# Sums over heads on TensorE: eight products dealt to four column strips

## What is computed

```python
kk = heads(k * k_k)
kk = kk / jnp.maximum(jnp.sqrt(jnp.sum(kk * kk, axis=-1, keepdims=True)), 1e-12)
...
mean = jnp.mean(y, axis=-1, keepdims=True)
var = jnp.mean(jnp.square(y - mean), axis=-1, keepdims=True)
y = ((y - mean) * lax.rsqrt(var + RWKV_LN_EPS)).reshape(bsz, seq, W) * ln_w + ln_b
bonus = jnp.sum(r * k * r_k, axis=-1, keepdims=True) * v
```

## Time and profile before

| what | before |
|---|---|
| time, median of 3 runs | 2844.51 us (2843.17 to 2844.96) |
| span of the profiled execution | 2846.5 us |
| TensorE busy, matmuls | 2803.9 us (99%) x17275 |
| VectorE busy | 1735.5 us (61%) |
| ScalarE busy | 1315.8 us (46%) |
| mean granted TensorE clock | 0.997 |
| instructions of `head_sum` (L804) | 64 matmuls, 64 weight loads |

### The profile page before, as it was taken

How to read it: one execution, slowest core, us unless ns; L and a number is a source line. 1 busy time by engine, 2 the same in 40 slices (tenths; PEclk the granted TensorE clock), 3 DMA queues, 4 the chain that set the end, 5 groups by cost and what they waited for, 6 DMA issues and landing times.

```text
span 2846.5 us, 40996 instructions
## 1 busy us (share of the span) xinstructions
PE 2803.9 (99%) x17275; PEld 2398.9 (84%) x17275; DVE 1735.5 (61%) x2053; ACT 1315.8 (46%) x1672; POOL 43.6 (2%) x71
## 2 busy tenths in 40 slices
PE   8999899999999999999999999999999999999998
PEld 7888788788888888888888888888888888888886
DVE  5688666654445555555555666655666756665665
ACT  6445333544434443444434545644554444443444
POOL 2000000000000000000000100000000000000001
PEclk9999999999999999999999999999999999999999
DMA  7565214555545656655666555555456555555553
GB/s 232 177 193 176 77 47 150 186 182 192 179 135 183 186 192 192 191 193 183 197 190 189 189 180 190 178 169 174 161 180 198 185 195 190 187 198 192 190 181 132
DMA packets 392420, 504.60 MB, mean 177 GB/s; under 512 B 11360, under 2 KB 285293, under 8 KB 391213
## 3 DMA queue, kind: packets, MB, share of 16 engines
q1 hardware_dynamic: 385149, 490.35, 53.5%
q10 hardware_dynamic: 7088, 11.62, 1.3%
HBM read 499.77 MB, written 2.17 MB: 176 GB/s over the span
## 4 chain that ended last, share of the span: by engine, by line
PE 95%; DVE 3%; ACT 1%; issue 1%; DMA 0%; ACTq 0%; SPq 0%; DVEq 0%
PE PS L639 37%; PE PS L644 33%; PE PS L648 17%; PE PS L864 3%; PE PS L676 1%; DVE wlo L1889 1%; PE PS L996 0%; PE PS L1012 0%; PE PS L804 0%; PE PS L784 0%; PE PS L1045 0%; DMA slab<-in_x 0%; ACT whi L1287 0%; PE PS L819 0%; PE PS L1036 0%
## 5 line engine op out<-in xcount | busy, mean ns | idle before, releaser
L1889 DVE TENSOR_TENSOR wlo<-raw,whi 128x1024 fp32r<-128x1024 f32 x922 | 1127.0, 1228 | 791.1 <-ACT whi L1287 787.5
L1287 ACT ACTIVATE whi<-raw 128x1024 fp32r<-128x1024 f32 x922 | 970.3, 1057 | 963.3 <-PE PS L648 497.9
L644 PE MATMUL PS<-XX,whi 128*128 128x512 f32 (+1 forms) x3856 | 1216.8, 397 | 0.0
L648 PEld LDWEIGHTS PS<-XX,wlo 128*128 128x128 f32 (+1 forms) x3856 | 724.5, 188 | 171.3
L648 PE MATMUL PS<-XX,wlo 128*128 128x256 f32 (+1 forms) x3856 | 759.7, 278 | 0.0
L639 PE MATMUL PS<-whi,act 128*128 128x512 f32 x2240 | 602.1, 391 | 0.0
L644 PEld LDWEIGHTS PS<-XX,whi 128*128 128x128 f32 (+1 forms) x3856 | 589.3, 189 | 2.8 <-DVE wlo L1889 0.6
L639 PEld LDWEIGHTS PS<-whi,act 128*128 128x128 f32 x2240 | 418.0, 188 | 85.3
L639 PE MATMUL PS<-wlo,act 128*128 128x512 f32 x1120 | 344.9, 389 | 0.0
L639 PE MATMUL PS<-whi,XX 128*128 128x512 f32 x1024 | 280.8, 396 | 6.5 <-DVE wlo L1889 5.1
L639 PEld LDWEIGHTS PS<-wlo,act 128*128 128x128 f32 x1120 | 210.2, 188 | 44.0
(11 more groups left out here) (363 smaller groups left out, 1355.5 us busy)
## 6 DMA issues: line engine op xcount, KB each, us to landing
raw<-in_ffn_w SPq DMA_DIRECT2D x128, 1024.0 KB, 5.5
raw<-in_w_in SPq DMA_DIRECT2D x103, 1024.0 KB, 5.0
raw<-in_w_ffn_gate SPq DMA_DIRECT2D x44, 1024.0 KB, 4.9
raw<-in_w_ffn_up SPq DMA_DIRECT2D x44, 1024.0 KB, 4.9
raw<-in_w_ffn_down SPq DMA_DIRECT2D x44, 1024.0 KB, 5.1
raw<-in_w_out SPq DMA_DIRECT2D x32, 1024.0 KB, 5.1
raw<-in_xattn_wk SPq DMA_DIRECT2D x16, 1024.0 KB, 5.2
raw<-in_xattn_wv SPq DMA_DIRECT2D x16, 1024.0 KB, 5.0
```

The costliest lines, as they stand in the source:

```text
L644: T.matmul(ps[0:wd, f, :], whi[:, o:o + wd], b.x[:, kk, :], start=first, stop=False, skip_group_check=True)
L648: mm = T.matmul(ps[0:wd, f, 0:SEQ], wlo[:, o:o + wd], b.x[:, kk, 0:SEQ], start=False, stop=last, skip_group_check=True)
L1287: S.activation(k.whi[:, h % 4, 0:b.size], k.raw[:, t % 4, u * b.size:(u + 1) * b.size], ACT.Copy).then_inc(k.w_hi, 1)
L1889: V.tensor_tensor(k.wlo[:, h % 4, 0:b.size], k.raw[:, h // 2 % 4, u * b.size:(u + 1) * b.size], k.whi[:, h % 4, 0:b.size].bitcast(F32), AL ...
```

## The change

`sel` becomes [128, 2, 32]. A product of the feature group 2q + b goes to PSUM partitions 32q to 32q + 31, q from 0 to 3, b from 0 to 1; the two products of a strip add up there. In 32 columns of `sel[:, b, :]` the columns 16b and 16b + 8 select the two heads of the group, so that head h stands on partition 8h. The other columns select windows of 64 partitions that lie across heads or are cut off; they are computed and not used. In program order b is the outer loop. `hs` and `bs` become all 128 partitions wide, the steps on them work on 128 partitions, and the stores take every eighth partition, 16 rows as before. The constant takes four selects in place of two.

```diff
-        self.sel = sb("sel", [P, RP, 16])
+        self.sel = sb("sel", [P, 2, 32])
...
-        self.hs, self.bs = v(23568, SEQ)[self.HP, :], v(23824, SEQ)[self.HP, :]
+        self.hs, self.bs = v(23568, SEQ), v(23824, SEQ)
...
 def head_sum(k, src, bank, n=SEQ):
 
-    for f in range(RP):
-        mm = k.nc.tensor.matmul(k.PS[k.HP, bank, 0:n], k.sel[:, f, :], src[:, f, :], start=f == 0,
-                                stop=f == RP - 1)
+    for b in range(2):
+        for q in range(4):
+            mm = k.nc.tensor.matmul(k.PS[32 * q:32 * q + 32, bank, 0:n], k.sel[:, b, :], src[:, 2 * q + b, :],
+                                    start=b == 0, stop=b == 1, skip_group_check=True)
     return mm
...
-    S.activation(k.hs, k.PS[k.HP, 4, 0:SEQ], ACT.Sqrt).then_inc(rp.act, 1)
+    S.activation(k.hs, k.PS[:, 4, 0:SEQ], ACT.Sqrt).then_inc(rp.act, 1)
...
-    S.dma_start(k.norms_out[0], k.hs).then_inc(k.norm_stored[0], 16)
+    S.dma_start(k.norms_out[0], k.hs[0:P:8, :]).then_inc(k.norm_stored[0], 16)
...
-    S.dma_start(k.bonus_out, k.bs).then_inc(k.bonus_stored, 16)
+    S.dma_start(k.bonus_out, k.bs[0:P:8, :]).then_inc(k.bonus_stored, 16)
...
-    S.dma_start(k.norms_out[1][:, P * h:P * h + P], hs).then_inc(k.norm_stored[1 + h], 16)
+    S.dma_start(k.norms_out[1][:, P * h:P * h + P], hs[0:P:8, :]).then_inc(k.norm_stored[1 + h], 16)
...
-    V.tensor_copy(bs, PS[k.HP, 4, 0:SEQ]).then_inc(rp.dve, 1)
+    V.tensor_copy(bs, PS[:, 4, 0:SEQ]).then_inc(rp.dve, 1)
...
-    R, VV, sums = k.RKV[:, 0:8, tok], k.RKV[:, 16:24, tok], k.PS[k.HP, 4 + 2 * h, 0:P]
+    R, VV, sums = k.RKV[:, 0:8, tok], k.RKV[:, 16:24, tok], k.PS[:, 4 + 2 * h, 0:P]
...
-    select(k.sel[:, :, :], [[128, RP], [-64, 16]], 0, 1, ge, 0.0)
-    select(k.sel[:, :, :], [[-128, RP], [64, 16]], 63, -1, ge, 0.0)
+    for b in range(2):
+        for lo, cm, st in ((128 * b, 1, -8), (63 - 128 * b, -1, 8)):
+            select(k.sel[:, b, :], [[st, 32]], lo, cm, ge, 0.0)
```

## The result

The changed kernel takes 2837.06 us (median of 6 runs, 2834.64 to 2838.56) where the kernel before took 2845.29 us beside it (6 runs, 2843.17 to 2845.96). The ratio is 0.9972, with a 95% interval of 0.9962 to 0.9981: faster by 0.28%, some 8 us. The forecast was 2837.3. The profiled executions span 2837.3 us after and 2846.5 before.

The account below looks back on a forecast made before the run. TensorE, busy 99% of 2846.5 us, was taken as the bound; 4.8 us from two 256-column calls and 2.45 from the post pair, 7.2 in all, off the 2844.5 median gave 2837.3. Range 2835.3 to 2839.2, with rivals 1 to 3 up to 2844.8.

Parts of the forecast that it names:

- What bounds the kernel: TensorE, busy 99% of the span; the head sums' three insertions of 3.74, 3.75 and 3.82 us count in full.
- (a): Head-sum products on TensorE: four strips stream at once, insertions of 1.34, 1.34 and 1.37 us, 7.2 us gained.
- (b): Going into and out of the narrow-column matmul form around each head-sum call on TensorE: stays 0.30 us.
- (c): Steps reading the sums, on 128 partitions instead of 16: no change, at most 0.1 us each, 0.2 us on the path.
- (d): Stores of the sums, sixteen rows from every eighth partition: post-stage landing unchanged at 4.1 us.
- (e): Four selects build the constant on GpSimd instead of two: at most 0.7 us more there, nothing on the path.
- Arrival: TensorE's gains pass VectorE's splits at all three places: 2.4, 2.4 and 2.45 us; chunk stage starts at about 299.6.
- The clock: The half-speed stretch after the post-stage stall stays as it is, plus or minus 2 us for a window.
- (1): Rival for the head-sum products: strips overlap only in pairs, 2.03 us a 256-column call, 2839.3 us in all; chance 0.15.
- (2): Rival for the head-sum products: strips sharing their rows do not overlap, nothing gained, 2844.5 us; chance 0.17.
- (3): Rival: half the gain lost to VectorE after the second call or to lower clock, 2840 to 2843 us; chance 0.12.
- (4): Rival: strips take turns and each of 29 strip changes costs 0.30 us, 8.7 us slower, 2853 us; chance 0.04.

Follow-up runs that it names:

- four_times: The changed kernel with each call's eight products issued four times over, the last round counting; 2844.72 us in one run.
- before_again: The kernel before, unchanged, run and profiled once more; 2845.41 us in one run.
- one_product: The changed kernel with one product over all 128 columns in place of each call's eight, sums not the reference's; 2833.41 us in one run.

## Why the prediction was right, step by step

**What bounds the kernel.** Right. Every insertion on TensorE counted in full in the time between halves, and the medians are 8.2 us and 8.1 us apart in the two series. 7.65 us from TensorE and 0.30 us from the post stage make 7.95; the 0.2 to 0.3 us that are left are not placed.

**(a) The products.** The mechanism was right, with one term too large. Expected 1.34, 1.34 and 1.37 us, measured 1.21, 1.21 and 1.24. The term is the late start of the fourth strip, 6 x 29 ns = 0.18 us: the strips start 7 ns apart, 0.02 us in all. The 29 ns of the earlier trace rows are what the quadrant products took each, 16 in 0.47 us, and I took them for the least time between two issues, which they are not. For the same reason the 128-column calls are set by streaming (0.87 us) and not by issue (0.93). The streaming terms, 0.86 and 0.87, were right. The gain is 7.65 us instead of 7.2.

The rule that spoke against the change did not hold. The Trainium skill, TensorE: Matmul & The Clock Gate, The mechanism, allows a weight load beside running matmuls only in another row group; here all 16 loads share their rows and overlap with matmuls and with one another, 0.59 us for 16 of 0.11 us. The efficiency of three column tiles in that page's section Measured speedup vs the span model is on the right side, but low for this case: my estimate from it was 1.1 us before the way in and out, and four_times shows 0.853 for each 16 passes, four times the rate of one strip.

**(b) The way in and out.** 0.30 us kept, 0.35 measured, and shown to be the change of form: without it the call takes 3.45 us, 0.00 over the streaming.

**(c) The readers.** That 128 partitions cost no more than 16 was right. That nothing changes was wrong, and this is the part of the mechanism that I missed: I had bounded the cost only from above and for the number of partitions, and had counted only L2252 and L2253 as standing on the path, when those of the post stage stand ahead of the stall at 500 us. The reciprocal of the earlier trace rows lasts 1.75 us and holds VectorE for 1.78 before the change (the next step starts at 176.14), where on partitions from 0 it is 1.68. After the first call the readers give back 0.3 us of VectorE, which no wait of TensorE's asks for (0.03 us there); in the post stage it is the 0.30 us of TensorE at half 109.

**(d) The stores.** Right. ScalarE's wait ahead of the squares, kernel after, against 3.89 in the earlier trace rows and 3.65 in before_again:

```profile
473.01 1.91 ACT L1394 ACTIVATE over_x<-slab 128x2048 f32<-128x2048 f32 x1 [3.67 <-issue]
```

The stores land in 4.0 us, 4.1 before.

**(e) The constants.** Right: GpSimd's four selects take 1.06 us from the first to the last, where the two took 0.75, and nobody waits for them.

**Arrival.** Right at all three places. The chunk stage starts at 299.67 us, 299.6 forecast, and this nearness is luck: 5.1 us were gained by then and not 4.8, and 0.3 lost to scatter ahead of half 30. The idle time of VectorE at 232.40 and 234.60 is gone, that at 224.04 and 256.89 has shrunk from 0.60 and 1.04 to:

```profile
221.71 0.69 DVE L1905 TENSOR_TENSOR slab<-PS,slab 128x512 f32<-128x512 f32 x1 [0.48 <-ACT slab L1324]
...
252.14 0.69 DVE L1905 TENSOR_TENSOR slab<-PS,slab 128x512 f32<-128x512 f32 x1 [0.55 <-ACT slab L1324]
```

The gain had room, but the working had the limit in the wrong place. I added up VectorE's three idle times from 232 us on, 2.45 us, and called that the room. The tightest place lies before them: the split of half 71, 2.49 us ahead before and 0.33 after. Up to there TensorE moved by 4.75 us and the split by 2.59, most of that from the first call. That the two rooms were alike, 2.45 and 2.49 us, was luck.

**The clock.** I left it as it is with plus or minus 2 us. In the pair of profiles 1.8 us came from it, by chance. The profile says 9.2 us and the medians 8.2, and this is most of the difference; whoever reads the span alone gives the change 1 us too much.

**The rivals.** (1) Two strips at a time fell: 2.03 us forecast for it, and a kernel with only two strips took 2.07, while four took 1.21. (2) No overlap fell with the first row of L805. (3) Nothing was taken back, but the second call was within 0.2 us of it, as one_product shows. (4) A change of strip costs nothing that can be seen: four_times has four times the changes of the kernel after, and each 16 passes more cost their streaming alone. The 0.30 us belong to a change of form, of which there is one pair for each call whatever the number of strips.

That the sum hit the median to 0.3 us was partly luck. The gain was forecast 0.75 us too small, 0.45 from TensorE and 0.3 from the readers, and it was taken off a median of before that was 0.8 us lower (2844.5, three runs) than the one measured beside the change (2845.3, six runs).

## What to carry to other kernels

Small products that contract over all 128 rows and fill few columns can be dealt to column strips: the time of the group is that of the fullest strip plus 0.35 us for one change of form, whatever the order of the products. Count what the other engines can spare behind each place before you count the gain, and look at the starts of VectorE's steps, not at their durations: here a small tile that begins at partition 32 or 96, between neighbours that begin at 0, costs about 0.1 us on the way there and again on the way back. Where one profile has a stretch at half clock that the other lacks, run the unchanged kernel again before giving it to the change.

## What was not expected of the hardware

- Four f32 products on the same rows and different columns run at full rate at once: 64 passes of 256 columns took 3.66 us, where 16 passes on one strip took 3.63.
- As far as start times tell, TensorE started a matmul of one strip ahead of nine earlier ones that waited for other strips; the worse order of the products costs 0.02 to 0.04 us a call.
- Going to another column form and back costs 0.30 to 0.35 us together; a 256-column call in the 128-column form, which the work around it has too, costs nothing beyond 16 x 0.216 us.
- VectorE loses about 0.1 us on the way to a step that starts at partition 96 or 32, and again behind it, between steps that start at 0; with a start at 0 it loses nothing, on 16 or 128 partitions.
- The same work in the chunk stage ran with nothing, 3.41 us or 6.83 us at the 1.2 GHz level, which made it 0, 1.8 or 3.4 us longer, from one execution to the next.
